# Modulation pieces multiplied and added up on VectorE beside the FFNs, in a two-block transformer kernel

## The reference, cut to what matters

```python
sc = jax.nn.silu(c)                                   # (1, 1024)
for i in range(2):
    mod = (sc @ ada_w[i] + ada_b[i]).reshape(B, 9, 1024)   # ada_w[i]: 1024 x 9216, fp32
    x = modulated_sublayer(x, mod[:, 0:3], g[0], g[1], ffn(i, 0), 0.5)
    x = modulated_sublayer(x, mod[:, 3:6], g[2], g[3], mixer(i), 1.0)   # pooling, then latent attention
    x = modulated_sublayer(x, mod[:, 6:9], g[4], g[5], ffn(i, 1), 0.5)

def modulated_sublayer(x, mod, g_pre, g_post, fn, weight):
    h = rmsnorm(x, g_pre) * (1.0 + scale) + shift
    return x + weight * (1.0 + gate) * rmsnorm(fn(h), g_post)
```

## Time and profile before

| what | value |
|---|---|
| median of three runs | 1854.14 us (1851.59 to 1854.83) |
| the profiled execution | 1848.86 us |
| its span, first to last instruction | 1847.0 us |
| mean granted TensorE clock | 0.955 of 2.4 GHz |
| DVE, ACT busy | 59%, 47% |
| read from memory | 371 MB, 202 GB/s over the span |

### The profile page before, as it was taken

One profiled execution on the slowest core, in us unless ns is written; L12 is line 12 of the kernel. 1 busy time (PEld: TensorE's weight loads), 2 busy tenths in 40 slices (PEclk: granted clock), 3 DMA queues, 4 the chain that ended last, 5 costly groups with the idle time before them and its releaser, 6 DMA issues.

```text
span 1847.0 us, 19745 instructions
## 1 busy us (share of the span) xinstructions
PE 1700.0 (92%) x7873; PEld 1289.2 (70%) x7873; DVE 1092.1 (59%) x1531; ACT 874.4 (47%) x1256; POOL 19.6 (1%) x39
## 2 busy tenths in 40 slices
PE   5999999899998999979899997999888778999997
PEld 1676766476776778856668886876667667777875
DVE  2545446564455545553555555577676647988886
ACT  2444333243344434435544444454544436767774
POOL 1000000000000000000000000000000000000000
PEclk9999999799999999999899999999789889999999
DMA  9777665646785585543265654444023136989993
GB/s 357 274 265 259 228 234 210 240 160 228 261 284 179 174 287 187 178 149 137 69 215 175 198 187 103 162 143 157 26 91 103 46 99 229 362 304 337 323 326 146
DMA packets 211313, 373.76 MB, mean 202 GB/s; under 512 B 8880, under 2 KB 102486, under 8 KB 211216
## 3 DMA queue, kind: packets, MB, share of 16 engines
q1 hardware_dynamic: 208368, 364.52, 57.8%
q0 software_dynamic: 2448, 6.82, 1.4%
q10 hardware_dynamic: 400, 1.10, 0.2%
HBM read 371.36 MB, written 1.05 MB: 202 GB/s over the span
## 4 chain that ended last, share of the span: by engine, by line
PE 82%; DVE 9%; ACT 5%; DMA 3%; issue 1%; SPq 0%; DVEq 0%; ACTq 0%
PE banks L516 22%; PE banks L518 21%; PE banks L517 21%; PE banks L557 2%; DVE ul L460 2%; PE banks L692 2%; DMA raw<-in_ada_w 2%; PE banks L577 1%; DMA raw<-in_ffn_w_in 1%; PE banks L550 1%; ACT uh L449 1%; PE banks L1200 1%; PE banks L1653 1%; ACT full L664 1%; PE banks L1173 1%; PE banks L2102 1%
## 5 line engine op out<-in xcount | busy, mean ns | idle before, releaser
L460 DVE TENSOR_TENSOR ul<-raw,uh 128x1024 fp32r<-128x1024 f32 (+2 forms) x548 | 659.8, 1212 | 449.8 <-ACT uh L449 441.8
L449 ACT ACTIVATE uh<-raw 128x1024 fp32r<-128x1024 f32 (+2 forms) x548 | 570.2, 1048 | 488.6 <-PE banks L518 376.9
L516 PE MATMUL banks<-uh,hh 128*128 128x512 f32 (+2 forms) x1280 | 528.0, 413 | 14.5 <-DVE hl L729 5.9
L518 PE MATMUL banks<-uh,hl 128*128 128x512 f32 (+2 forms) x1280 | 503.1, 393 | 0.0
L517 PE MATMUL banks<-ul,hh 128*128 128x512 f32 (+2 forms) x1280 | 502.1, 392 | 0.0
L516 PEld LDWEIGHTS banks<-uh,hh 128*128 128x128 f32 x1280 | 245.4, 192 | 93.5 <-issue 27.4
L517 PEld LDWEIGHTS banks<-ul,hh 128*128 128x128 f32 x1280 | 245.8, 192 | 53.3 <-issue 7.7
L518 PEld LDWEIGHTS banks<-uh,hl 128*128 128x128 f32 x1280 | 245.0, 191 | 52.1
L516 PE MATMUL banks<-uh,bh 128*128 128x512 f32 x528 | 211.8, 401 | 16.1 <-DVE bl L858 8.1
L518 PE MATMUL banks<-uh,bl 128*128 128x512 f32 x528 | 207.6, 393 | 0.0
L517 PE MATMUL banks<-ul,bh 128*128 128x512 f32 x528 | 207.2, 392 | 0.0
(11 more groups left out here) (300 smaller groups left out, 1332.1 us busy)
## 6 DMA issues: line engine op xcount, KB each, us to landing
raw<-in_ffn_w_in SPq DMA_DIRECT2D x176, 512.0 KB, 6.2
raw<-in_ada_w SPq DMA_DIRECT2D x72, 1024.0 KB, 7.0
raw<-in_w_up SPq DMA_DIRECT2D x64, 1024.0 KB, 5.6
raw<-in_ffn_w_out SPq DMA_DIRECT2D x44, 1024.0 KB, 9.8
raw<-in_w_down SPq DMA_DIRECT2D x32, 1024.0 KB, 5.6
raw<-in_w_in SPq DMA_DIRECT2D x22, 1024.0 KB, 5.1
raw<-in_w_mem_kv SPq DMA_DIRECT2D x4, 1024.0 KB, 10.3
raw<-in_mla_w_o SPq DMA_DIRECT2D x4, 1024.0 KB, 5.0
```

The lines of the kernel that those rows point to most:

```text
L449: act.e.activation(uh[r][:, 0:w], raw[m % NRAW][:, h * w:(h + 1) * w], AF.Copy).then_inc(act_done, ta.put("hi", u))
L460: dve.e.tensor_tensor(ul[r][:, 0:w], raw[m % NRAW][:, h * w:(h + 1) * w], uh[r][:, 0:w].bitcast(F32), ALU.subtract).then_inc(dve_done, tv. ...
L516: pe.e.matmul(o, a, wh, start=s0, stop=False)
L518: mm = pe.e.matmul(o, b, wh, start=False, stop=s1)
```

## The change

Nineteen pieces, those beside the FFNs (ADA_AT), are no longer multiplied on PE. DVE multiplies and adds the eight slices into one of two accumulators `acc` in SBUF (128 x 512): one `tensor_scalar` and seven `scalar_tensor_tensor`, four per chunk, each waiting for the one before. These are `later` steps in the block after `side(b)`: with the weights 1.4, 1.4, 1.4 and 0.1 the first four run behind its first unit, the other four behind its second. DVE's fourth and eighth operation free the slots; `may_split` and `stream` follow that (`given`, `by_dve`). PE sums a piece over partitions one piece later, behind the first unit of the block after (`sum_due_pe`), or when the queue is flushed at the FFN's end; DVE ends it one or two units after that.

For all 36 pieces the bias moves from the products to the sum, and the sum of a shift or scale piece ends in columns: four matmuls with the partial sums as weights and one column of `sum4` or of ones, and four with the bias as weights. DVE's end for these is one operation of 128 x 4. ACT's copy falls away for the nineteen, and so do ACT's waits in `side`. There is no new transfer; `ones` is a memset at the start.

```diff
 def stream(sp, lo, hi):
...
+                    elif m - NRAW in by_dve:
+                        sp.wait_ge(dve_done, tv("raw", m - NRAW))
...
 def may_split(eng, upto):
...
-            m = units[u][0]
-            return m < NRAW or chunks[m - NRAW][4] or eng.chunk_at > m - NRAW
+            m = units[u][0] - NRAW
+            if m < 0 or chunks[m][4]:
+                return True
+            return m in eng.given if m in by_dve else eng.chunk_at > m
...
+        def ada_sum_pe(pe, a, b, part, pick):
...
+            if kind == 2:
+                pe.e.matmul(PB[b], pick, part, start=True, stop=False)
+                mm = pe.e.matmul(PB[b], ident[0:36, r:r + 1].to_broadcast([36, P]), adab[0:36, :], start=False,
+                                 stop=True)
+            else:
+                for k in range(4):
+                    o = PB[b][:, k:k + 1]
+                    pe.e.matmul(o, part[:, k * P:(k + 1) * P], pick[:, 0:1], start=True, stop=False)
+                    mm = pe.e.matmul(o, adab[0:36, k * P:(k + 1) * P], ident[0:36, r:r + 1], start=False, stop=True)
...
+        def ada_beside_pe(pe, a):
+            yield 1.4
+            yield 1.4
+            sum_due_pe(pe)
+            yield 1.4
+            pe.sum_due = a
+            yield 0.1
...
+        def ada_beside_dve(dve, a):
+            got = [take_raw(dve, ("ada",) + a) for _ in range(2)]
+            dst = ada_acc(a)
+            for k in range(KD):
+                m, w = got[k // 4]
+                if k % 4 == 0:
+                    yield 1.4
+                dve.wait_ge(ring[m % NRAW], landed[m])
...
+                    add = dve.e.tensor_scalar(dst, w[:, 0, :], sc[:, 0:1], None, ALU.mult)
+                else:
+                    dve.own()
+                    add = dve.e.scalar_tensor_tensor(dst, w[:, k % 4, :], sc[:, k:k + 1], dst, ALU.mult, ALU.add)
...
+                    add.then_inc(dve_done, tv.put("raw", m))
+                    dve.given.add(m)
+                if k == 3:
+                    yield 1.4
+            tv.same("acc", a)
+            yield 0.1
+            sum_due_dve(dve)
+            dve.sum_due = a
...
 def sub_ffn_pe(pe, i, s, gap=(), between=nothing):
...
-                    ada_pe(pe, ADA_AT[i, s, b])
+                    for _ in range(2):
+                        take_raw(pe, ("ada",) + ADA_AT[i, s, b])
+                    pe.later.add(ada_beside_pe(pe, ADA_AT[i, s, b]))
...
-            pe.later.flush()
+            flush_pe(pe)
...
 def sub_ffn_act(act, i, s, gap=(), between=nothing, first=False):
...
-                    act.wait_ge(dve_done, tv("tl", q, 3))
-                    if b and (i, s, b - 1) in ADA_AT:
-                        act.wait_ge(pe_done, tp("ada_t", ADA_AT[i, s, b - 1]))
-                    ada_act(act, ADA_AT[i, s, b])
+                    act.later.add(ada_beside_act(act, ADA_AT[i, s, b]))
```

More of the change, by code:

```diff
@@ L309, in build @@
         spare = [AR[:, XN_END + n * 512:XN_END + n * 512 + 512] for n in range(2)]
+        acc = [AR[:, XN_END + 2176 + n * 512:XN_END + 2176 + n * 512 + 512] for n in range(2)]
+        ones = AR[:, ARENA - P:ARENA]
         wide_bufs = [flat2(ug[0][:, :, :]), flat2(ug[1][:, :, :]), flat2(sg[:, :, :])]
@@ L398, in build @@
         ring = [sem(f"ring{i}") for i in range(NRAW)]
+        beside = set(ADA_AT.values())
+        by_dve = {m for m, c in enumerate(chunks) if c[0][0] == "ada" and c[0][1:] in beside}
         landed, fills = [], [0] * NRAW
@@ L543, in ada_parts_pe @@
         def ada_parts_pe(pe, a, b):
-            i, j = a
-            r = i * 18 + j
-            got = [take_raw(pe, ("ada", i, j)) for _ in range(2)]
-            pe.wait_ge(loaded("ident"), 16)
-            pe.wait_ge(loaded("ada_b"), 16)
+            got = [take_raw(pe, ("ada",) + a) for _ in range(2)]
             pe.take(b)
-            pe.e.matmul(PB[b][0:32, :], ident[0:36, r:r + 1].to_broadcast([36, 32]), adab[0:36, :],
-                        start=True, stop=False)
             pe.wait_ge(act_done, ta("sc"))
@@ L575, in ada_total_pe @@
             pe.wait_ge(loaded("sum4"), 16)
-            pe.take(b)
-            pe.e.matmul(PB[b], sum4[:, :], buf, start=True, stop=True).then_inc(pe_done, tp.put("ada_t", a))
-            pe.frees(b, dve_done, tv, "ada_e", a)
+            ada_sum_pe(pe, a, b, buf, sum4[:, :])
         def ada_end_dve(dve, a, b):
-            i, j = a
-            s, kind, half = i * 3 + j // 6, (j // 2) % 3, j % 2
+            r, s, kind, half = ada_place(a)
             dve.wait_ge(pe_done, tp("ada_t", a))
+            dst = None if kind == 2 else ab[:, s, 1 - kind, half * 4:half * 4 + 4]
             if kind == 2:
@@ L610, in end_step_dve, with ada_acc @@
             ada_end_dve(dve, a, b)
[L613 to L624 removed]
+        def ada_acc(a):
+            return acc[ADA_ORDER.index(a) % 2]
@@ new lines, in sum_due_pe, with sum_due_dve @@
+        def sum_due_pe(pe):
+            a, pe.sum_due = pe.sum_due, None
+            if a is not None:
+                pe.wait_ge(dve_done, tv("acc", a))
+                ada_sum_pe(pe, a, 7, ada_acc(a), ones)
+        def sum_due_dve(dve):
+            a, dve.sum_due = dve.sum_due, None
+            if a is not None:
+                ada_end_dve(dve, a, 7)
+        def ada_beside_pe(pe, a):
[5 more added lines that the diff above has]
+            yield 0.1
@@ new lines, in ada_beside_act @@
+        def ada_beside_act(act, a):
+            got = [take_raw(act, ("ada",) + a)[0] for _ in range(2)]
+            yield 1.4
+            act.given.add(got[0])
+            yield 1.4
+            yield 1.4
+            act.given.add(got[1])
+            yield 0.1
[5 more added lines that the diff above has]
+                if k % 4 == 0:
+                    yield 1.4
+                dve.wait_ge(ring[m % NRAW], landed[m])
+                if k == 0:
+                    before = ADA_ORDER[ADA_ORDER.index(a) - 2]
+                    if before in beside:
+                        dve.wait_ge(pe_done, tp("ada_t", before))
+                    dve.wait_ge(act_done, ta("sc"))
+                    add = dve.e.tensor_scalar(dst, w[:, 0, :], sc[:, 0:1], None, ALU.mult)
+                else:
+                    dve.own()
+                    add = dve.e.scalar_tensor_tensor(dst, w[:, k % 4, :], sc[:, k:k + 1], dst, ALU.mult, ALU.add)
+                if k % 4 < 3:
+                    add.then_inc(dve_done, tv.put())
+                else:
+                    add.then_inc(dve_done, tv.put("raw", m))
+                    dve.given.add(m)
+                if k == 3:
+                    yield 1.4
+            tv.same("acc", a)
+            yield 0.1
+            sum_due_dve(dve)
+            dve.sum_due = a
@@ L627, in gap_copies_act, with flush_pe, flush_dve @@
+        def flush_pe(pe):
+            pe.later.flush()
+            sum_due_pe(pe)
+        def flush_dve(dve):
+            dve.later.flush()
+            sum_due_dve(dve)
         def gap_copies_act(act, pieces):
@@ L764, in pre_dve @@
         def pre_dve(dve, s, gap=(), first=False):
-            dve.later.flush()
+            flush_dve(dve)
             if not first:
@@ L977, in start_dve @@
             dve.e.memset(hp[:, :, 264:272], 0.0).then_inc(dve_done, tv.put())
+            dve.e.memset(ones, 1.0).then_inc(dve_done, tv.put())
         def mem_norm_act(act):
```

49 lines of the change are left out of this document (20 added, 29 removed).

## The result

The changed kernel took 1972.24 us (median; 1968.72 to 1978.53) against 1854.49 for the kernel before on the same chip: a ratio of 1.0637, 95% interval [1.0601, 1.0673]. The forecast was 1930 with a range of 1878 to 1952. The direction and the mechanism held, the size didn't, and the time lies above the range. The profiled execution took 1968.72 us, its span is 1966.9, its mean granted clock 0.924.

The account below looks back on a forecast made before the run. PE, busy 92% of the span, was taken as the bound, with late bl stalling it after the change. Six items summed to +76 us on 1848.9 profiled: 1925, or 1930 for the median; range 1878 to 1952.

Parts of the forecast that it names:

- Item 1: Sixteen FFN blocks with pieces before and behind: 25.3 us each, PE stalled on late bl; +69.5 us in all.
- the in-block part of item 3: One in-block sum per FFN not hidden in a stall, so exposed on PE: +2.7 us.
- The clock in item 1: After each gated block's stall PE runs at the low clock, costing 1.6 us of work per block.
- The rival in which the clock holds: No low clock after stalls, or quicker landing and additions: 1905 us, 1890 with landing at 4.6 also; chance 0.26.
- Item 2: First piece of each of three FFNs leaves PE, 2.85 us each, with no gated block behind: -8.6 us.
- Item 3: PE's column and gate sums take 1.8 us instead of 0.9, hidden in gated blocks; exposed +2.7 and +6.3 us.
- Item 4: The 17 other pieces: dearer sums, less the bias gone from their products mostly beside PE's waits; +3.4 us.
- Item 5: Start: four column sums in a row delay PE, DVE's end steps get shorter; +1 us, bounds 0 and 3.6.
- Item 6: Memory norm's steps in FFN (0,0) fall behind the stall: +2 us, range 0 to 4.
- the flush of item 3: Each FFN's last sum, behind its last down matmul, with DVE's end step ahead of the post-norm: +6.3 us.
- The faster one: Rival: the slot's later release does no harm, blocks take PE's own 18.8 us; 1826 us, chance 0.10.
- Dearer: Rival: additions of 1.0 us or more each, or dearer stalls, make blocks of 29 us; 1960 us, chance 0.08.

Follow-up runs that it names:

- e10: e9 with shift and scale pieces beside the FFNs summed in columns, eight one-column matmuls each; 1852.71 us.
- e6: Kernel before with only the bias matmul of all 36 pieces moved from the products to the sum, over rows; 1884.76 us.
- e2: Changed kernel with all sums over rows again and DVE's old end, bias still at the sum, additions still on DVE; 1971.49 us.
- e5: Changed kernel for the nineteen pieces only; the 17 others exactly as before, bias with the products and row sum; 1939.85 us.
- e9: Changed kernel with DVE's eight additions ahead of the block's own down units, row sums for all, 17 other pieces as before; 1838.78 us.
- e12: e9 with the first piece's sum behind its block's third unit, and four-matmul column sums for shift and scale among the 17 others; 1829.27 us.
- e7: Kernel before with column sums of four one-column matmuls for shift and scale pieces, bias left with the products; 1849.74 us.

## Why the prediction was wrong in size, by its own steps

**Item 1, the gated blocks (+69.5): right.** Every step of the worked block was met within 0.1 us, but for the wait: 4.56 instead of 4.9, since PE's own work ended at 13.7 and not 13.3 (143.43 - 4.56 - 125.20); the gate sum ahead of it took 2.1 us and not 1.8. The additions took 752 ns (0.78 forecast with the wait), the first product 0.48 (0.5), the landing 5.5 (5.5). Over all, the three FFN stretches grew by 73.6 us, where items 1, 2, 6 and the in-block part of item 3 had 69.5 - 8.6 + 2 + 2.7 = 65.6. The other 8 us are mostly in FFN (0,1), +27.0, with blocks of 24.9 to 28.3: in the one of 28.3 PE stood 6.75 us before bl, not 4.6. The nine intervals from the first transposes of FFN (0,0) on are 23.4 to 27.2 us, 25.8 in the mean, so 25.3 was half a microsecond low.

**The clock in item 1: right.** The forecast took 1.6 us for each stall from a single case. From the down matmuls to the block's end it was 150.51 - 143.43 = 7.08 us, where 5.5 is the full clock's: 1.6. It is the repeating case that the trace before lacked: 0.50 for 144 to 146 us and for parts of its neighbours. The trace after has sixteen such stalls of 2.2 to 6.8 us ahead of down matmuls; at fourteen of them the low clock follows, at the two shortest (2.17 and 2.48 us) it doesn't. By the rule of the Trainium skill ("TensorE: Matmul & The Clock Gate", HAM oscillation) bursts parted by waits start at the low clock each time, and the trace agrees for these fourteen. The rival in which the clock holds is out.

**Item 2 (-8.6)** can't be read by itself: what the first pieces gave back is inside the +73.6.

**Item 3, the sums: mis-sized.** A column sum was 1.8 us in the forecast, worked out from records of 36 columns. It took 2.4 in the blocks (153.23 to 155.61), and at the start 16 records at half rate, 4.1 us a piece. The nearest row was of another shape. Worse, the term was priced as PE time only. That the clock falls behind it, with no wait of PE just ahead, as at 156.87 after and at 118 in e10, was in no term.

**Item 4, the 17 other pieces (+3.4): the step that failed.** It read "the bias gone from their products, mostly beside PE's waits (-3, bounds 0 and -17)". Taking work out beside a wait was priced as a small gain, and putting it back behind the sum at 0.9 us for six pieces and +1 for all others. e6 does this for all 36 pieces and measures +30 us. At the start the bias matmul filled pauses of PE; without it PE ran at half rate through all the products, and in e6 through the sums too. Ahead of the four stages the bias matmuls of two pieces each lay in a wait for DVE where they cost nothing; the waits grew by 9.4 us in all (9.3 in the changed kernel), and the matmuls came back where PE is the bound. The forecast asked what PE waits for, and not what fills its waits.

**Item 5, the start (+1, bounds 0 and 3.6): wrong by the rate.** It was +10.1. The four column sums lasted 16.5 us (36.43 to 52.9), not four times 1.8, because they ran at half rate. Row sums in their place, which came back to the full rate, leave +2.8 (e2); row sums that didn't cost 12.1 (e6). So the loss is that of the half rate, with either form of sum.

**Item 6 (+2)** was not tested.

Summed up: items 4, 5 and the flush of item 3 (6.3) gave 10.7 us for the stretches between the FFNs, and 46.2 were measured. The 35.5 between them and the FFNs' 8 are the miss. e5, in which the 17 pieces are left alone, has +8.5 there instead of 46.2 and took 1939.85 us, within 10 us of the forecast; its FFNs (+75.6) are still 10 above the sum.

**The rivals.** The faster one (slot released early enough, 18.8 us a block, 1826) wasn't what the change does, but its block was right: e9 and e12 are that kernel, with blocks of 19.0 and 1838.78 and 1829.27 us. "Dearer" (1960) had a time near the result and the wrong reason: no addition took 1.0 us.

## What to carry to other kernels

A look-ahead that runs in program order turns a buffer that comes free late into a stall of whatever stands behind it, so when a ring slot's last user changes engine, work out when the slot comes free, which queue waits for its next content, and what lies behind that wait; if it's late, release earlier rather than reorder one consumer. A small matmul that stands in a wait costs nothing there, so before moving it ask where it goes: behind the wait it costs its own time. And look at the duration of the matmuls around it at both rates: it may be what brings TensorE to its full clock, and then it costs far more. Price a matmul of few columns from a row of its own shape, and look at the rate of what follows it.

## What was not expected of the hardware

- The granted clock fell without any idle time of PE: behind eight matmuls of one column (16 records, 2.4 us), in e10 at 118 us and in five more of its ten in-block sums, and after at 156.87. Four of them (8 records) didn't do it in e7's FFN blocks, but four such sums in a row did at its start; sums over rows (e9) didn't do it in any block. Why some and not others was not separated.
- At the start PE ran at half rate in e6 and after for every chunk (1.93 us for 8 records, against 1.06), and through the sums for 16 us more of uninterrupted work, though PEclk reads 1.00 there. The trace's list of clock levels begins with the first full clock: at 26.3 us before, 38.5 in e2, 57.9 after and 58.2 in e6, and the durations shorten there (in e6 transposes of 0.42 us become 0.28 at 58.2). Up to there the 1.00 is the absence of an entry, and the duration of a repeated instruction is the witness.
- Code that no kernel changed, from the last transposes of FFN (1,1) to the end, takes 713 us in the profiled executions of before and after, and 720 to 721 in those of e5, e6, e9 and e12. It is again the clock: 0.50 for 104 us of it before and for 122 in these four. The same 60 us of it in before and in e9 (us, PE busy, PEclk, DMA share, GB/s):

```profile
1302.50:1362.50 60.00, 52.17 (x213) 0.73 0.15 47
```

```profile
1285.00:1345.00 60.00, 54.69 (x198) 0.60 0.09 28
```

That is why differences here are read by stretch, and spans only where they exceed some 8 us.
